# Seventeen of 22 gate and up pairs as seven block products for eight in a two-layer decoder trunk

## What is computed

```
def _swiglu(hn, w_gate_up, w_down):
    gu = hn @ w_gate_up
    gate, up = jnp.split(gu, 2, axis=-1)
    return (jax.nn.silu(gate) * up) @ w_down

# per layer, with hn = rmsnorm(h): h = h + rmsnorm(_swiglu(hn, ...))
# per sample row and head (chunk length 1):
#   S_new = S * exp(g) + k (outer) v        # returned as gdn_sample, ret_sample
```

## Time and profile before

| quantity | value |
|---|---|
| three executions | 1433.58, 1434.93, 1436.19 us |
| span of the profiled execution, first to last instruction | 1431.1 us |
| PE busy | 1413.0 us, 99%, 12580 matmuls |
| PEld busy | 1390.9 us, 97% |
| DVE busy | 850.7 us, 59% |
| ACT busy | 544.2 us, 38% |
| POOL busy | 99.7 us, 7% |
| mean granted TensorE clock | 0.996 |
| DMA, mean over the span | 103 GB/s |

### The profile page before, as it was taken

How to read it: one execution, slowest core, us unless ns; L and a number is a source line. 1 busy time by engine, 2 the same in 40 slices (tenths; PEclk the granted TensorE clock), 3 DMA queues, 4 the chain that set the end, 5 groups by cost and what they waited for, 6 DMA issues and landing times.

```text
span 1431.1 us, 29170 instructions
## 1 busy us (share of the span) xinstructions
PE 1413.0 (99%) x12580; PEld 1390.9 (97%) x12580; DVE 850.7 (59%) x1393; ACT 544.2 (38%) x1050; POOL 99.7 (7%) x141
## 2 busy tenths in 40 slices
PE   9999999999999999999999999999999999999997
PEld 8999999999999999999989999999999999999996
DVE  7745895877555554332486569868775555543224
ACT  5135463556222222322342364643652222232222
POOL 0001211100000000000000012111000100000000
PEclk9999999999999999999999999999999999999998
DMA  5332332122343343222213313412323333322221
GB/s 202 108 103 71 97 114 81 60 89 81 111 142 137 139 136 119 89 89 94 84 60 112 110 60 97 120 60 74 96 74 121 137 140 137 137 97 89 92 100 61
DMA packets 57695, 147.45 MB, mean 103 GB/s; under 512 B 19040, under 2 KB 22496, under 8 KB 57568
## 3 DMA queue, kind: packets, MB, share of 16 engines
q1 hardware_dynamic: 49744, 119.89, 24.9%
q0 software_dynamic: 7824, 25.70, 5.0%
HBM read 132.79 MB, written 12.78 MB: 102 GB/s over the span
## 4 chain that ended last, share of the span: by engine, by line
PE 92%; DVE 5%; ACT 1%; issue 1%; DMA 0%; SPq 0%; DVEq 0%; ACTq 0%
PE PS L577 77%; PE PS L583 5%; DVE hT L1664 1%; DVE Wl L1626 1%; DVE Xl L1643 1%; DVE mT L1663 1%; PE PS L771 1%; PE PS L1100 1%; PE PS L755 0%; PE PS L917 0%; PE PS L743 0%; PE PS L753 0%; PE PS L822 0%; PE PS L596 0%; PE PS L1021 0%
## 5 line engine op out<-in xcount | busy, mean ns | idle before, releaser
L577 PE MATMUL PS<-Xh,Wh 128*128 128x260 f32 x2464 | 504.2, 286 | 2.6 <-DVE Xl L1685 2.2
L577 PE MATMUL PS<-Xl,Wh 128*128 128x260 f32 x2464 | 497.8, 283 | 0.0
L577 PE MATMUL PS<-Xh,Wl 128*128 128x260 f32 x2464 | 495.9, 283 | 0.0
L1168 ACT ACTIVATE Wh<-stage 128x1024 fp32r<-128x1024 f32 x211 | 223.6, 1060 | 661.9 <-PE PS L577 643.7
L577 PEld LDWEIGHTS PS<-Xh,Wh 128*128 128x128 f32 x2464 | 382.3, 189 | 7.6 <-DVE Xl L1685 2.6
L577 PEld LDWEIGHTS PS<-Xh,Wl 128*128 128x128 f32 x2464 | 379.9, 188 | 0.0
L577 PEld LDWEIGHTS PS<-Xl,Wh 128*128 128x128 f32 x2464 | 379.6, 189 | 0.0
L1626 DVE TENSOR_TENSOR Wl<-stage,Wh 128x1024 fp32r<-128x1024 f32 x211 | 257.9, 1222 | 181.8 <-ACT Wh L1168 181.3
L577 PE MATMUL PS<-actH,Wh 128*128 128x260 f32 x616 | 124.1, 283 | 0.0
L577 PE MATMUL PS<-actH,Wl 128*128 128x260 f32 x616 | 124.0, 282 | 0.0
L577 PE MATMUL PS<-actL,Wh 128*128 128x260 f32 x616 | 123.7, 282 | 0.0
(11 more groups left out here) (327 smaller groups left out, 1600.5 us busy)
## 6 DMA issues: line engine op xcount, KB each, us to landing
stage<-w_slabs SPq DMA_DIRECT2D x211, 512.0 KB, 3.3
dst<-state_ret POOLq DMA_DIRECT2D x32, 256.0 KB, 3.2
dst<-state_gdn POOLq DMA_DIRECT2D x32, 256.0 KB, 3.1
out_gdn_sample<-dst POOLq DMA_DIRECT2D x16, 256.0 KB, 2.8
out_ret_sample<-dst POOLq DMA_DIRECT2D x16, 256.0 KB, 3.1
hT<-x_t SPq DMA_DIRECT2D x3, 520.0 KB, 7.0
out_y_t<-hT SPq DMA_DIRECT2D x3, 520.0 KB, 3.0
hT<-x_t SPq DMA_DIRECT2D x2, 260.0 KB, 3.6
```

Of the source, the lines that this page charges most:

```text
L577: ins = mm(pj(slot)[:, a], w[:, ws, pos, :], x[:, a, :], start=first and w is Wh and x is xh, stop=last and w is Wl)
L1168: A(Wh[:, G % NW], stage[:, G % NS], ACT.Copy).then_inc(s["hi_split"], 1)
```

## The change

Pairs 0 to 4 (`NP` = 5) stay as they are. For pairs 5 to 21 (`Q` = 17, numbered q) the eight block products (2 tiles x 2 halves of the 1024 features x 2 halves of the columns) are made as seven products of sums of blocks (Strassen's scheme, the form with 15 additions). Each is 4 blocks x 3 passes = 12 matmuls of 260 columns.

- The seven sums on the activation side are made once a layer, as copies of `hT` with the weight on ScalarE (`weighted`) and steps of VectorE (`x_scaled`, `x_sum`, `x_low`) among pairs 0 to 4. They hold `rb` too, so those outputs aren't scaled when they are taken out.
- The seven sums on the weight side are made for each pair. SP loads quarters of 256 KB: b11 to two slots with one broadcasting DMA, b2 (the up tile's second half) to two slots, one plain (`quarters`). GpSimd adds a fourth quarter to two of these slots by DMAs with `accum_op`. VectorE makes two more sums (`w_sum2`, `w_sum4`), ScalarE rounds (`w_high`), VectorE subtracts (`w_low`). Three sets of buffers are used: the first pair's lies in free memory of the mixer, the odd pairs' over `stage`, `Wh` and `Wl`, the even pairs' over `Xl` and `Xh`.
- The seven products are added up in three PSUM banks, and five steps of VectorE (`post`), a copy (`first_copy`) and two Silus of a half each on ScalarE take them out. `actF` holds the product unsplit; all 22 are split at the end of the last pair (`act_high`, `rest_act`).
- The rows' transposes, `value_block`, `outer`, `new_state` and GpSimd's stores move from the gate and up stage to the slabs of the down stage.
- Some semaphores are merged (seven for the statistics into `stats_ready`, `kqpad_zeroed` into `x_zeroed`; the wait for `rb_ready` in `outer` is gone).

```diff
+            def quarters(l, q):
+                N = l * Q + q
+                w = w_set(q)[2]
+                if q == 0:
+                    sp.wait_ge(s["state_stored"], (l + 1) * 32)
+                elif q < 3:
+                    sp.wait_ge(s["tile_done"], l * TILES + T_DN)
+                else:
+                    sp.wait_ge(s["p_done"], (N - 2) * UN + US1 + 1)
...
+                sp.dma_start(w[:, UA11:US1 + 1:2], quarter(l, q, 0, 0).unsqueeze(1).to_broadcast([P, 2, QW])).then_inc(s["b11_loaded"], 16)
+                if q >= 3:
+                    sp.wait_ge(s["p_done"], (N - 2) * UN + US4 + 1)
...
+                sp.dma_start(w[:, US3:US4 + 1], quarter(l, q, 1, 1).unsqueeze(1).to_broadcast([P, 2, QW])).then_inc(s["b2_loaded"], 16)
+                sp.dma_start(w[:, UA12], quarter(l, q, 0, 1)).then_inc(s["b2_loaded"], 16)
...
+                    if n == S_DN:
+                        for q in range(Q):
+                            quarters(l, q)
+                        sp.wait_ge(s["p_done"], (l * Q + Q - 1) * UN)
...
+                for q in range(Q):
...
+                    pool.wait_ge(s["b11_loaded"], (N + 1) * 16)
+                    pool.dma_start(w[:, US1], quarter(l, q, 1, 0), accum_op=ALU.add).then_inc(s["t1_summed"], 16)
...
+                    pool.wait_ge(s["b2_loaded"], (N + 1) * 32)
+                    pool.dma_start(w[:, US3], quarter(l, q, 1, 0), accum_op=ALU.add).then_inc(s["t3_summed"], 16)
...
+                def strassen(q):
+                    N = l * Q + q
+                    lo_, hi_, full = w_set(q)
+                    a_, b_, c_ = acc_banks(q)
+                    for u, bank in enumerate((a_, b_, c_, a_, b_, c_, b_)):
...
+                        if u % 2 == 0:
+                            pe.wait_ge(s["ffn_rest"], l * REST + X_STEPS + q * W_STEPS + W_LO + u // 2)
...
+                        elif u == UA12:
+                            pe.wait_ge(s["gate_half"], N * HALVES + P1_COPY)
+                        elif u == US3:
+                            pe.wait_ge(s["post_done"], N * POSTS + U2)
+                        elif u == US4:
+                            pe.wait_ge(s["post_done"], N * POSTS + TD)
+                        elif u == UA22:
+                            pe.wait_ge(s["post_done"], N * POSTS + C22)
+                        for k in range(4):
+                            cols = slice(k * P, (k + 1) * P)
+                            mm(PS[:, bank, 0:HC], hi_[:, u, cols], XU[:, u, 0, k], start=k == 0 and u < 3, stop=False, skip_group_check=True)
+                            mm(PS[:, bank, 0:HC], hi_[:, u, cols], XU[:, u, 1, k], start=False, stop=False, skip_group_check=True)
+                            ins = mm(PS[:, bank, 0:HC], lo_[:, u, cols], XU[:, u, 0, k], start=False, stop=k == 3, skip_group_check=True)
+                        ins.then_inc(s["p_done"], 1)
...
-                    if i >= 6 and i % 2 == 0 and i < 38:
-                        outer((i - 6) // 2)
...
+                        if b == 7:
+                            rows_back()
+                        elif b % 8 == 7 and 2 <= b // 8 < 18:
+                            outer(b // 8 - 2)
...
+                    if j == 0:
+                        for k in range(KT):
+                            weighted(k)
                     act.wait_ge(s["tile_free0"], (T0 + T_GU + 2 * j) // 2 + 1)
...
+                    if q + 1 < Q:
+                        w_high(q + 1, 0)
+                        w_high(q + 1, 1)
+                        gate_first(q)
+                        w_high(q + 1, 2)
+                        w_high(q + 1, 3)
...
+                def w_sum2(q):
+                    N = l * Q + q
+                    w = w_set(q)[2]
+                    dve.wait_ge(s["t1_summed"], (N + 1) * 16)
+                    dve.wait_ge(s["b2_loaded"], (N + 1) * 32)
...
+                    V.tensor_tensor(w[:, US2], w[:, US1], w[:, US4], ALU.add).then_inc(s["ffn_rest"], 1)
...
+                    freed(V.tensor_tensor(gp, pj(3 if j == 1 else 0), rb[:], ALU.mult), t)
+                    if j and 2 * j + NW < 2 * NP:
                         lo(G0 + S_GU + 2 * j + NW)
...
+                    if j == 0:
+                        x_scaled(0)
...
                     done(t + 1)
...
+                    freed(V.tensor_tensor(up, pj(1), rb[:], ALU.mult), t + 1)
...
+                    if j == 0:
+                        x_scaled(1)
+                        x_scaled(2)
...
+                    else:
+                        for c in range(3):
+                            w_low(0, c)
...
+                for q in range(Q):
+                    last = q == Q - 1
+                    if q:
+                        post(q - 1, C21)
+                    w_low(q, 3)
+                    if q:
+                        gated(q - 1)
+                    if not last:
+                        w_sum2(q + 1)
+                    else:
+                        rest_act(0, 2)
+                    post(q, U2)
+                    if not last:
+                        w_sum4(q + 1)
+                    else:
+                        rest_act(2, 2)
+                    post(q, TD)
+                    if not last:
+                        w_low(q + 1, 0)
+                        w_low(q + 1, 1)
+                    else:
+                        lo(G0 + S_DN)
+                        rest_act(4, 2)
+                    post(q, C22)
+                    if not last:
+                        w_low(q + 1, 2)
+                    else:
+                        rest_act(6, 2)
+                    post(q, C12)
...
                     lo(G0 + S_DN + i + NW)
...
+                    if 1 <= i < 17:
+                        value_block(i - 1)
...
+                    if 2 <= i < 18:
+                        new_state(i - 2)
```

More of the change, by code:

```diff
@@ L250, in trunk, with w_set, acc_banks, plain @@
         B_V = (6, 4, 5, 6)
-        vblks = [vblk0[:], vblk[:]]
+        vblks = [vblk[:, 0], vblk[:, 1]]
+        gp, up = (sqb[:, i].rearrange("p (a n) -> p a n", a=2) for i in range(2))
+        def w_set(q):
+            return (loC, hiC, fullC) if q == 0 else (loB, hiB, fullB) if q % 2 else (loA, hiA, fullA)
+        def acc_banks(q):
+            return (0, 1, 2) if q % 2 else (4, 5, 6)
+        def plain(ap):
+            return ap.bitcast(fp32)
+        def x_full(u):
+            return XF[:, u, 1]
+        def act_full(j):
+            return actF[:, j] if j < FT - 2 else (act20, act21)[j - FT + 2][:]
+        def act_low(j):
+            return actL[:, j] if j < FT - 2 else actL2[:, j - FT + 2]
+        def quarter(l, q, up_, k):
+            return w_slabs[l, S_GU + 2 * (NP + q) + up_, :, k * QW:(k + 1) * QW]
         QR = 32
@@ L412, in slab @@
                     sp.wait_ge(s["lo_split"], G - NS + 1)
-                sp.dma_start(stage[:, G % NS], w_slabs[l, n].rearrange("p (k n) -> p k n", k=KT)).then_inc(s[f"slab{G % NS}_loaded"], 16)
+                sp.dma_start(stage[:, G % NS], w_slabs[l, n if n < S_DN else n + 2 * Q].rearrange("p (k n) -> p k n", k=KT)).then_inc(s[f"slab{G % NS}_loaded"], 16)
             def x_part(i, k0, k1):
@@ L1102, in _ @@
                 first_halves(2, S_GU, T_GU)
-                for i in range(3, 2 * FT):
+                for i in range(3, 2 * NP):
                     wait_slab(l, S_GU + i)
@@ L1552, in _, with weighted @@
                 second_x(2)
+                def weighted(k):
+                    if k == 0:
+                        act.wait_ge(s["h_ready"], nth_norm(l, 2))
+                    row = R_FPRE + k
+                    first = (UA11 if k < 4 else UA12) * 8 * HC + 4 * HC + k % 4 * HC
+                    second = US4 * 8 * HC + k % 4 * HC if k < 4 else UA22 * 8 * HC + 4 * HC + k % 4 * HC
+                    to = bass.AP(XF, first, [[XU_N, P], [second - first, 2], [1, HC]])
+                    A(to, hT[:, k], ACT.Copy, scale=prm[:, l, row:row + 1]).then_inc(s["ffn_round"], 1)
@@ L2168, in _ @@
+                lo(G0 + S_DN + 1)
+                rest_act(8, 2)
+                post(Q - 1, C21)
+                rest_act(10, 2)
+                gated(Q - 1)
+                rest_act(12, 2)
+                lo(G0 + S_DN + 2)
+                for j in range(14, FT - 2, 2):
+                    rest_act(j, 2)
+                rest_act(FT - 2, 1)
+                rest_act(FT - 1, 1)
                 step(V.memset(ss[:], 0.0))
```

366 lines of the change are left out of this document (283 added, 83 removed).

## The result

The changed kernel takes 1450.0 us (median; 1448.9 to 1450.7) beside 1434.3 us for the kernel before, a ratio of 1.0119 (95% interval 1.0107 to 1.0132). The forecast was 1407, with a range of 1398 to 1427. The profiled execution's span is 1448.7 us, 17.6 more than before.

The account below looks back on a forecast made before the run. TensorE was taken as the bound, 99% busy, 0.12 us a matmul. 48.9 us saved less 11.4 (stage start), 8.6 (first pair) and 0.8 (last pair) gave 28.1, so 1434.9 became 1407 us, range 1398 to 1427.

Parts of the forecast that it names:

- The matmuls taken away: Changed gate and up pairs: 84 matmuls for 96 over 34 pairs, pitch of 0.12 us kept, 48.9 us saved.
- The start of the stage: Gate and up start: TensorE idle 4.4 us behind x_scaled(0), plus 1.3 for the slow clock; 11.4 us lost over two layers.
- The first changed pair: First Strassen pair: waits for w_low(0,0), then for the second pair's load and accumulation; 4.3 us a layer, 8.6 in all.
- The steady pairs: Pairs after the first: 10.06 us each, w_sum2 needed by +3.9 with data landing about then; cost taken as 0.
- The bound of 15 us: Steady pairs: most that late batches, landing up to +5.0, could cost over 28 pairs; kept for the range.
- Rival A: Changed pairs: crowded DMA queues, share 0.69, batches landing near +5, 14 us lost; 1421 us (1413 to 1428), chance 0.21.
- d = x/2: Steady pairs: a batch late by x stalls each pair by d, half of x, since the stall also delays the next pair.
- Rival B: Changed pairs: accumulating transfer is the bound, stalls from 6.0 us, gain gone at 7.6; slower, 1475 at 10 us; chance 0.12.
- The last pair: Last changed pair: C22 runs behind lo and two rest_act, 0.4 us a layer, 0.8 in all; down stage's start costs nothing.
- the state updates: Moved from gate and up to down stage: 32 outer products of 0.25 us before and after, move costs nothing.
- the stores behind the accumulations: GpSimd's queue: stores stand behind the layer's 34 accumulating transfers, the last issued before the down stage; no cost.
- The semaphores and the mixer: Merged semaphores cost nothing, each still waiting for the same event; second layer's mixer counted at 0.

Follow-up runs that it names:

- e6_dvesum: Changed kernel with four plain 256 KB loads a pair and VectorE making the two sums instead of accumulating transfers: 1407.5 us, ratio 0.9826 to the kernel before.
- e4_edges: Changed kernel with weighted copies, scaled copies and sums reordered in the plain pairs, two weight splits ahead of the last evacuation: 1438.4 us, ratio 1.0044.
- e1_plain: Changed kernel with both accumulating transfers of each changed pair made plain 256 KB loads, two weight sums left out: 1428.9 us, ratio 0.998.
- e7_states: Kernel before with only the transposes, value blocks, outer products and new states moved to the down stage: 1431.3 us, ratio 0.9998.
- e2_absent: Changed kernel with the accumulating transfers left out, waiters waiting for the load before them, two weight sums missing: 1407.8 us, ratio 0.9832.
- e8_best: e6_dvesum with the order of e4_edges and, in the first changed pair, two product steps ahead of the second pair's weight sums: 1394.8 us, ratio 0.9736.

## Why the prediction was wrong, point by point

**The matmuls taken away: right.** 12172 instead of 12580, and the pitch of 0.12 us held with all twelve in one bank. `e6_dvesum` has pairs of 10.09 us for the 10.06 that I gave.

**The start of the stage: right.** Forecast was TensorE at 347.4 after 4.4 us; it was 347.21, after 4.46 us more than before. The granted clock then read 0.50 until 351.7, and tile 3 took 7.83 us for 5.84, 2.0 longer, for the 1.3 that I added; in the second layer it took 7.15 for 5.83, 1.3 longer. `e4_edges` removed the pause and was 10.7 us faster than the changed kernel.

**The first changed pair: the term was half of what it measured**, 17.2 us for 8.6. The start at +2.9 was exact. What failed is the landing: I had the quarters after 3.6 us and the accumulation after 4.0 more, and it was 4.9 (389.84 to 394.75) and 6.2 (394.75 to 400.95). My working forgot what sets out at the same time. The second pair's own second batch of 768 KB is issued at 390.25 and 390.76, within 1 us of its first quarters, and the third pair's loads follow from 394.28 on: they too wait for no product, only for the last plain tile and the load before them. The slow clock behind the first pause fell into the wait, as I had said; in the first layer it fell again behind the second pause (0.50 from 402.92 to 406.33) and cost some 1.6 us more. In the second layer a second pause of 2.12 us had none.

**The steady pairs: here the sign was lost**, 35.6 us for 0. The working of the order was right to the tenth: `w_sum2` must start by +3.9, and where it starts at +3.82 (pair 9) the pair takes 10.12, at +6.16 (458.23 less 452.07, pair 5) 12.47, that is 2.3 late and 2.4 longer. The step that failed is "lands +3.1; with the accumulation crossing ... +3.9 to +4.6". It added the accumulation's bytes to the stream at the best rate. From the copies' issue to GpSimd's next issue, which waits for both loads, that is 4.3 us, with the crossing 5.1 to 5.8; the first layer's pairs 3 to 16 have 5.4 to 7.7 us, 6.9 in the mean. The bound of 15 us rested on the same sentence.

**Rival A was the right mechanism, with the wrong size.** It forecast a share of 0.69, measured 0.67, and from that a batch at +5 and 1421 us. The share was right and the delay was not: a mean share of 0.67 is not evenly spread. The batch goes out together with one accumulating transfer and just ahead of another, and each waits for the other's packets. A mean landing near +6.3 would give the measured 1.2 us a pair by the same d = x/2.

**Rival B was the right sign for a reason that was half wrong.** It had the accumulating transfer as the bound beyond 6.0 us and break-even at 7.6 (its own formula gives 7.5). That transfer is not slow alone: where the queues are nearly empty, in the first pair's own set, its median landing, and that of the plain load in its place in `e1_plain`, are

```profile
fullC<-w_slabs POOLq DMA_DIRECT2D x4, 256.0 KB, 3.8
```

```profile
fullC<-w_slabs POOLq DMA_DIRECT2D x4, 256.0 KB, 2.8
```

3.8 us, for the 4.0 that I had taken, and 1.0 more than plain. It is slow in company, 5.8 and 5.1 us in the median, over 8 at the worst; the one ahead of `w_sum2` lasted over the 6.0 us of the forecast's own warning in 10 of the 28 pairs. And as `w_sum2` waits for both, the batch was late as often as the sum. I gave A and B a chance and a price as if only one could come; they are one mechanism, and it hits the first pair too. The upper end of A, 1428, and the first pair's 8.6 us too many together make 1437, which is in the range of B.

**The last pair, the state updates, the stores behind the accumulations: right.** Down took 131.57 us for 127.6, the 16 outer products of 0.25 and no more, and `e7_states` has a ratio of 0.9998.

**The semaphores and the mixer: 1.3 us, open.** In the second layer's mixer the changed kernel waits once for a step of ScalarE,

```profile
928.50 0.66 PE L891 MATMUL PS<-cf,vT 128*128 128x128 f32 x4 [1.10 <-ACT bv L1481]
```

and so do all its eight variants, the fastest too; the kernel before and `e7_states` don't. It isn't the move of the states, then. What else it is wasn't tried; the merged semaphores, which I put at nothing, are among what is left.

## What to carry to other kernels

A transfer that gets a new neighbour is priced by what is under way when it is issued, not by the mean share of the queues: list for each batch everything that goes out within its own landing time, count an accumulating transfer at more than twice a plain one's time in the queues (1.63 us for 0.73), and see how long after its due time the last of them may come. Where an engine's order leaves 0 to 1 us of slack for such a landing, take the stall as the likeliest case. Two additions a pair on an engine with slack, 0.61 us each, and four plain loads were worth 42 us here against two accumulating transfers and two doubled loads; the doubled loads by themselves had fitted (`e2_absent`). And before a sum goes to GpSimd, look whether VectorE runs steps with two operands in SBUF at the time.

## What the runs showed that I had not expected

- An accumulating transfer of 256 KB took the 16 DMA engines 1.63 us, a plain one 0.73; alone it landed in 3.8 us (plain 2.8), beside a batch of 768 KB in 8.0.
- Moving one load of 256 KB ahead by two products, with all transfers the same, was worth 20 us in 1450.
- VectorE, with two operands in SBUF, and GpSimd shut each other out: a multiply of 0.69 us took 1.79 behind a sum, and a sum of 1.31 took 1.76 behind a multiply. And two sums on GpSimd cost more than the same two on VectorE, which was already busy three quarters of the time.
- TensorE's pauses of much the same length were not always followed by the slow clock. Behind those of 2.71 and of 4.64 to 6.76 us in the gate and up stages the granted clock read 0.50 each time in all the traces; behind the 2.07 us in the changed kernel's first layer it did too, behind the 2.12 in its second layer, the 2.01 of `e8_best` and a pause of 2.42 at the start of `e6_dvesum` it did not. So an execution can be a few microseconds longer for that alone.
